# Modulation vectors summed wholly on VectorE, and gate rows spread over the partitions through DRAM

## Chip, cores and metric

One core of one Trainium2 chip. The metric is the device time of the program in microseconds; three runs of a kernel are shown by their median.

## What is computed

Two models run one after the other on 256 tokens of width 1024. The first has two layers of feed-forward, a mixer (state-space, mLSTM and RWKV heads side by side) and feed-forward. The second takes its output and a context of 256 more tokens through two layers. Before each of its parts the rows are normalised, scaled and shifted, and each part's output is multiplied by a gate. All scales, shifts and gates of a layer are the nine parts of one vector of 9216 numbers, and there are two such vectors, one for the tokens (from `c`), one for the context (from `c_ctx`):

```python
silu_c, silu_cc = jax.nn.silu(c), jax.nn.silu(c_ctx)
for l in range(2):
    m_lat = jnp.split(silu_c @ ada_w[l] + ada_b[l], 9)      # ada_w[l]: 1024 x 9216
    m_ctx = jnp.split(silu_cc @ ada_w[l] + ada_b[l], 9)
    def half_ffn(t, m, j):
        h = rmsnorm(t, norm_g[l, j]) * (1 + m[3*j + 1]) + m[3*j]
        return t + 0.5 * m[3*j + 2] * swiglu(h, ...)
    x, ctx = half_ffn(x, m_lat, 0), half_ffn(ctx, m_ctx, 0)
    ...                                                     # Fourier mixing (l=0) or retention (l=1), gated by m[5]
    x, ctx = half_ffn(x, m_lat, 2), half_ffn(ctx, m_ctx, 2)
```

In layer 1 the context ends with retention. Everything is float32. Products are made from a high part and a low part of each operand, three matmuls for one.

## The kernel before

The program is a list of stages (`network`, line 2926): f10 (first feed-forward of layer 0), the mixer, f20, f11, the mixer, f21, then half00, four (Fourier), half02, half10, ret (retention), retout, half12. A stage has phases. `run` in `network` appends a phase to one order, and every engine emits its part of each phase in that order (`Core.run`, 337), so the place of a `run` sets the order on all engines. An engine runs its own queue in order and waits on semaphores of the others. On VectorE and ScalarE each instruction also waits for the one before it.

**Weights.** SyncE loads tiles of 128x2048 (1 MB) into eight places (`Core.fetch`, 319), as each place is released. ScalarE writes the high part of a tile (`split_hi`, line 310), VectorE the low part (`split_lo`, line 316). `Core.plan` puts each split at a position of the order: as early as the target for the high part is free. There are two such targets, three in the stages of 256 rows.

**Feed-forward** (`Ffn`). Each of 22 gate/up tiles is 48 matmuls (line 100), of 256 columns in f10 to f21 and half12 and 512 columns in half00, half02 and half10. Then ScalarE takes Silu of the gate part (line 860), VectorE multiplies by the other part (line 886), ScalarE writes the high part (864) and VectorE the low part (888). The down products follow, in two portions in the stages of 512 columns. `Gated.vector` (710) multiplies the result by the gate and adds it to the rows (712).

**Modulation vectors** (`Ada`). The weights stand with the 1024 inputs on the partitions. A tile holds 4 groups of 128 inputs by 512 outputs; two tiles give 512 outputs. For each group and each of the two vectors VectorE adds weights times one scalar per partition to `acc` (461 for the first, 464 for the rest: `scalar_tensor_tensor`, 128x512). After two tiles TensorE sums `acc` over the partitions, with eight matmuls that have 128 columns of `acc` as weights and a column of ones as input. VectorE adds the bias (`bias`, 474) into `mods`, with outputs on the partitions. The bank that TensorE writes is one that the running stage doesn't use (`ada_bank`), and `clear` makes it wait for the bias add before the bank is used again.

72 tiles are cut into 144 phases of four VectorE instructions, and a last one. `ffn` in `network` puts them between the phases of the feed-forward stages: in f10, f20, f11 and f21 beside two of three gate/up tiles and beside five of the down tiles, 20 in each stage; in half00 two beside every gate/up tile, 44; the rest in half02.

**Gates** (`Gates`). A gate vector is needed along the free dimension, the same on every partition. For each half row of 512 VectorE makes four diagonal 128x128 matrices (667), TensorE multiplies ones by them (four matmuls), and ScalarE copies the bank to `gb` (691). In the feed-forward stages one half row goes behind each of the first tiles.

**Start.** `Setup.scalar` loads the masks and small rows on ScalarE's queue (412 to 415) and takes Silu of the two vectors from the constants (416, 128x16). `Setup.vector` waits for these loads.

## Time and profile before

| | |
|---|---|
| median of 3 runs | 3445.48 us (3442.11 to 3447.05) |
| profiled execution, span | 3442.6 us (the page gives no other time of it) |
| TensorE matmul busy | 3305.7 us, 96% |
| VectorE busy | 2101.4 us, 61% |
| ScalarE busy | 1308.7 us, 38% |
| `scalar_tensor_tensor` of the sum, x504 | 379.0 us |
| first instruction of the sum in a pair of tiles, x72 | 35.1 us |
| DMA | 463.08 MB, mean 135 GB/s |

A busy share is an average over the whole span. Matmuls overlap, so TensorE's 96% doesn't say that it is never waiting. Which engine sets the pace has to be read stage by stage, from the distance between equal instructions and from what ended the idle time in front of them.

### The profile page before, as it was taken

How to read it: one execution, taken by the hardware profiler on the slowest of the kernel's cores; microseconds unless marked ns; L12 is line 12 of the kernel's file. 1: busy time of each engine (PE TensorE's matmuls, PEld its weight loads, DVE VectorE, ACT ScalarE, POOL GpSimd, SP SyncE). 2: the span in 40 equal slices, each digit the busy share in tenths (PEclk: the TensorE clock that was granted, in tenths of full speed). 3: DMA queues.
4: the chain of work that ended last, by engine and by line, in shares of the span. 5: the costliest groups of instructions: out<-in, count | busy, mean ns of one | idle time of the engine just before them, and what ended most of it. 6: DMA issues, size and time to landing. Idle time of an engine off the chain costs nothing.

```text
span 3442.6 us, 47741 instructions
## 1 busy us (share of the span) xinstructions
PE 3305.7 (96%) x19896; PEld 2886.8 (84%) x19896; DVE 2101.4 (61%) x2545; ACT 1308.7 (38%) x1584; POOL 115.9 (3%) x126
## 2 busy tenths in 40 slices
PE   7998999999999899999999999999999999999998
PEld 7988887998988888798888877888878888787897
DVE  6767657777776667678774855763353333544654
ACT  4444244444435234544421223322232222444443
POOL 0001200000000211000000000000000000000000
PEclk9999999999999999999999999999999999999999
DMA  6542021565553022455443531343222222323452
GB/s 247 235 178 74 27 96 67 204 239 197 236 208 117 27 71 74 171 230 217 147 165 122 179 119 38 134 141 104 87 93 90 93 97 73 126 99 109 165 184 98
DMA packets 83842, 463.08 MB, mean 135 GB/s; under 512 B 7573, under 2 KB 11285, under 8 KB 43562
## 3 DMA queue, kind: packets, MB, share of 16 engines
q1 hardware_dynamic: 77952, 451.45, 35.9%
q10 hardware_dynamic: 5674, 8.57, 0.8%
q8 instruction: 157, 2.57, 0.3%
q14 instruction: 59, 0.48, 0.0%
HBM read 458.95 MB, written 1.05 MB: 134 GB/s over the span
## 4 chain that ended last, share of the span: by engine, by line
PE 66%; DVE 24%; ACT 6%; issue 2%; DMA 0%; POOL 0%; DVEq 0%; ACTq 0%; POOLq 0%
PE ps L100 66%; DVE lo L316 8%; DVE acc L464 5%; ACT hi L310 3%; PE ps L557 1%; DVE acc L461 0%; DVE m0restMs L2004 0%; DVE m1restMs L2004 0%; DVE xt L712 0%; DVE ct L712 0%; DVE half00fin L710 0%; DVE f20rot L886 0%; DVE f21rot L886 0%; DVE f10rot L886 0%; DVE f11rot L886 0%
## 5 line engine op out<-in xcount | busy, mean ns | idle before, releaser
L316 DVE TENSOR_TENSOR lo<-raw,hi 128x2048 fp32r<-128x2048 f32 (+1 forms) x357 | 809.6, 2268 | 627.9 <-ACT hi L310 606.2
L310 ACT ACTIVATE hi<-raw 128x2048 fp32r<-128x2048 f32 (+1 forms) x357 | 676.0, 1894 | 578.1 <-PE ps L100 547.5
L464 DVE SCALAR_TENSOR_TENSOR acc<-raw,sil,acc 128x512 f32<-128x512 f32 x504 | 379.0, 752 | 20.4
L100 PE MATMUL ps<-half00hs,hi 128*128 128x512 f32 x672 | 209.4, 393 | 0.9 <-DVE lo L316 0.9
L100 PE MATMUL ps<-half02hs,hi 128*128 128x512 f32 x672 | 209.1, 392 | 1.0 <-DVE lo L316 1.0
L100 PE MATMUL ps<-half10hs,hi 128*128 128x512 f32 x672 | 208.5, 391 | 1.0 <-DVE lo L316 1.0
L100 PEld LDWEIGHTS ps<-half10hs,hi 128*128 128x128 f32 x672 | 125.7, 188 | 28.5 <-DVE lo L316 1.9
L100 PEld LDWEIGHTS ps<-half02hs,hi 128*128 128x128 f32 x672 | 125.5, 188 | 28.6 <-DVE lo L316 1.9
L100 PEld LDWEIGHTS ps<-half00hs,hi 128*128 128x128 f32 x672 | 125.1, 188 | 28.0 <-DVE lo L316 1.8
L100 PE MATMUL ps<-half02hs,lo 128*128 128x512 f32 x352 | 137.9, 392 | 0.0
L100 PE MATMUL ps<-half00hs,lo 128*128 128x512 f32 x352 | 137.6, 391 | 0.0
L100 PE MATMUL ps<-half10hs,lo 128*128 128x512 f32 x352 | 137.5, 391 | 0.0
L100 PE MATMUL ps<-half12hs,hi 128*128 128x256 f32 x704 | 127.2, 283 | 2.1 <-DVE half12hs L636 2.1
L100 PE MATMUL ps<-hi,half00hf 128*128 128x512 f32 x352 | 110.7, 394 | 2.1 <-DVE mods L474 1.4
L100 PE MATMUL ps<-hi,half02hf 128*128 128x512 f32 x352 | 110.4, 394 | 1.5 <-DVE mods L474 1.5
L100 PEld LDWEIGHTS ps<-half12hs,hi 128*128 128x128 f32 x704 | 109.3, 191 | 3.0 <-DVE half12hs L636 1.8
L100 PE MATMUL ps<-hi,half10hf 128*128 128x512 f32 x352 | 109.2, 390 | 0.0
L100 PE MATMUL ps<-f10hs_h,hi 128*128 128x256 f32 x352 | 101.5, 288 | 7.3 <-DVE lo L316 7.2
L100 PE MATMUL ps<-f21hs_h,hi 128*128 128x256 f32 x352 | 100.9, 287 | 5.5 <-DVE lo L316 3.8
L100 PE MATMUL ps<-msk 128*128 128x128 f32 x886 | 104.5, 276 | 1.0 <-PE ps L2819 1.0
L100 PEld LDWEIGHTS ps<-msk 128*128 128x128 f32 x886 | 102.4, 192 | 3.3 <-PE ps L2819 1.2
L100 PE MATMUL ps<-f20hs_h,hi 128*128 128x256 f32 x352 | 100.8, 286 | 3.2 <-DVE f20hs_l L636 1.5
(921 smaller groups left out, 8019.5 us busy)
## 6 DMA issues: line engine op xcount, KB each, us to landing
raw<-in_ffn_w_gate_up SPq DMA_DIRECT2D x88, 1024.0 KB, 9.0
raw<-in_ffn_gu SPq DMA_DIRECT2D x88, 1024.0 KB, 4.8
raw<-in_ffn_w_down SPq DMA_DIRECT2D x85, 1024.0 KB, 5.2
raw<-in_ada_w SPq DMA_DIRECT2D x72, 1024.0 KB, 4.9
raw<-in_w_in_t SPq DMA_DIRECT2D x28, 1024.0 KB, 4.9
raw<-in_ret_w_in SPq DMA_DIRECT2D x24, 1024.0 KB, 4.8
raw<-in_w_out SPq DMA_DIRECT2D x16, 1024.0 KB, 4.9
raw<-in_w_in_n SPq DMA_DIRECT2D x12, 1024.0 KB, 4.8
```

What stands on the lines that cost most here:

```text
L100: return p().matmul(o, l, r, start=start, stop=stop, skip_group_check=True)
L310: a().activation(self.high(w), self.raw[self.place(r)][:, 0:width], ACT.Copy).then_inc(*a.mark(self.wac, w))
L316: v().tensor_tensor(self.low(w), self.raw[self.place(r)][:, 0:width], self.high(w).bitcast(F32), ALU.subtract).then_inc(*v.mark(self.wdv, w))
L464: v().scalar_tensor_tensor(out=acc[:, n, :], in0=w[:, k, :], scalar=s, in1=acc[:, n, :], op0=ALU.mult, op1=ALU.add).then_inc(*v.mark(self. ...
L557: x = p().transpose(b[:, t * 128:(t + 1) * 128], self.xs[:, 2 * s + t, c * 128:(c + 1) * 128], K.ident)
```

## The change

The weights of `Ada` are laid out with the outputs on the partitions: a tile is two groups of 128 outputs by 1024 inputs. The two vectors come as rows of 1024 on every partition (`silb`, loaded by a broadcast of 8 KB to 128 partitions on ScalarE's queue), and Silu is taken there over 128x2048. One `scalar_tensor_tensor` with `accum_out` multiplies 128x1024 weights by a vector and sums over the inputs into one column of `mods`; a phase is two of them. The bias is added once per layer. TensorE has no part in it, nor have the banks and `clear`.

A gate takes one VectorE instruction (`gcol`, 128x16), one DMA per vector from `gcol` to a row in DRAM, where the 8 numbers of a partition go to places 128 elements apart, and one DMA that reads the row back to all partitions. ScalarE issues all of them: the writes in the first of two phases, and in the second it waits for the writes and issues the read. The second phase stands behind the second tile. The other hunks pass the arguments along, number the wait on `mods` by layer, and run two phases for each gate.

```diff
-        self.sil = m.take("sil", 8, 2)
+        self.gcol = m.take("gc", 2, 8)
         self.st = m.take("st", 512)
-        self.acc = m.take("acc", 2, 512)
+        self.silb = m.take("silb", 2, 1024)
+        self.prod = m.take("prod", 1024)
         self.free, self.end = m.at, END
...
-        a().activation(K.sil, K.cc2, ACT.Silu).then_inc(*a.mark(self.ac, "sil"))
+        a().dma_start(K.silb, A["c_c2"].broadcast_to([P, 2048]).rearrange("p (n k) -> p n k",
+                                                                           n=2)).then_inc(*self.c.mark())
+        a.wait_ge(*self.c.all)
+        a().activation(K.silb, K.silb, ACT.Silu).then_inc(*a.mark(self.ac, "sil"))
         yield
...
-    phases = 2 * 2 * 18 * 2 + 1
+    phases = 2 * 36 * 2
     def __init__(self, K, setup):
         super().__init__(K, "ada", "ada")
-        self.setup, self.reduced = setup, 0
+        self.setup = setup
         for i in range(72):
-            l, t, h = i // 36, i // 2 % 18, i % 2
-            self.tiles[2 * i] = [(K.A["ada_w_2"][l, t, h], 2048)]
-        self.banks = []
+            self.tiles[2 * i] = [(K.A["ada_w_2"][i // 36, i % 36], 2048)]
     def vector(self, v):
-        K, acc = self.K, self.K.acc
+        K = self.K
         v.wait_ge(*self.setup.ac["sil"])
         for i in range(72):
-            t, h = i // 2, i % 2
-            w = K.raw[K.place(self.mine[i])].rearrange("p (k n) -> p k n", k=4)
-            for k in range(4):
-                if k % 2 == 0 and (i, k) != (0, 0):
-                    yield
-                if h == 0 and k == 0 and t:
-                    self.bias(v, t - 1)
+            l, t = divmod(i, 36)
+            w = K.raw[K.place(self.mine[i])].rearrange("p (m k) -> p m k", m=2)
+            for m in range(2):
                 v.wait_ge(*K.landed(self.mine[i]))
                 for n in range(2):
-                    s = K.sil[:, 4 * h + k, n:n + 1]
-                    key = ("tile", i) if (k, n) == (3, 1) else ("sum", i, k, n)
-                    if h == 0 and k == 0:
-                        v().tensor_scalar(acc[:, n, :], w[:, k, :], s, None,
-                                          ALU.mult).then_inc(*v.mark(self.dv, *key))
-                    else:
-                        v().scalar_tensor_tensor(out=acc[:, n, :], in0=w[:, k, :], scalar=s, in1=acc[:, n, :],
-                                                 op0=ALU.mult, op1=ALU.add).then_inc(*v.mark(self.dv, *key))
...
+                    key = ("tile", i) if (m, n) == (1, 1) else ("sum", i, m, n)
+                    v().scalar_tensor_tensor(out=K.prod, in0=w[:, m, :], scalar=1.0, in1=K.silb[:, n, :], op0=ALU.mult,
+                                             op1=ALU.mult,
+                                             accum_out=K.mods[:, l, 2 * t + m, n:n + 1]).then_inc(*v.mark(self.dv, *key))
+                if (t, m) == (35, 1):
+                    v().tensor_tensor(K.mods[:, l], K.mods[:, l], bl(K.ab2[:, l, :], 2),
+                                      ALU.add).then_inc(*v.mark(self.dv, "mods", l))
                 yield
-    def clear(self, p):
-        if self.reduced:
-            p.wait_ge(*self.dv["mods", self.reduced - 1])
...
         K = self.K
         for _ in self.rows:
             yield
-        K.ada.clear(p)
         if self.idle:
             if len(self.rows) == 4 and not self.turn[0]:
                 self.before[0].row(p, 0, 1)
...
 class Gates(Stage):
-    def __init__(self, K, who, after, l, j, n, half, gb, dg, bank):
+    phases = 2
+    def __init__(self, K, who, after, before, l, j, n, half, gb):
         super().__init__(K, "gate", who, after)
-        self.l, self.j, self.rows, self.phases, self.half = l, j, 2 * n, 2 * n + 1, half
-        self.gb, self.dg, self.bank = gb, dg, bank
+        self.before, self.l, self.j, self.n, self.half, self.gb = before, l, j, n, half, gb
+        self.row = K.nc.dram_tensor(who + "row", (n, 1024), F32, kind="Internal").ap()
+        self.out, self.back = Loads(K.sem(who + "out"), n), Loads(K.sem(who + "back"))
     def vector(self, v):
+        K, at = self.K, 8 * (3 * self.j + 2)
+        if self.before:
+            v.wait_ge(*self.before.out.all)
+        v.wait_ge(*K.ada.dv["mods", self.l])
+        v().tensor_scalar(K.gcol, K.mods[:, self.l, at:at + 8, :].rearrange("p c n -> p n c"), self.half, None,
+                          ALU.mult).then_inc(*v.mark(self.dv, "gc"))
+        yield
+        yield
+    def scalar(self, a):
         K = self.K
-        self.enter(v)
-        v.wait_ge(*K.ada.dv["mods", 18 * self.l + 17])
-        for i in range(self.rows):
-            n, q = i // 2, i % 2
-            if i:
-                v.wait_ge(*self.pe["sum", i - 1])
-            for m in range(4):
-                c = 8 * (3 * self.j + 2) + 4 * q + m
-                v().tensor_scalar(self.dg[:, m, :], K.ident, K.mods[:, self.l, c, n:n + 1], self.half, ALU.mult,
-                                  ALU.mult).then_inc(*v.mark(self.dv, "dg", i, m))
-            yield
-        yield
-    def tensor(self, p):
-        b = self.K.ps[self.bank]
-        self.enter(p)
-        yield
-        for i in range(self.rows):
-            p.wait_ge(*self.dv["dg", i, 3])
-            if i:
-                p.wait_ge(*self.ac["gb", i - 1])
-            for m in range(4):
-                x = mm(p, b[:, m * 128:(m + 1) * 128], self.K.ones, self.dg[:, m, :])
-            x.then_inc(*p.mark(self.pe, "sum", i))
-            yield
-    def scalar(self, a):
         self.enter(a)
-        yield
-        for i in range(self.rows):
-            n, q = i // 2, i % 2
-            a.wait_ge(*self.pe["sum", i])
-            a().activation(self.gb[:, n, q * 512:(q + 1) * 512], self.K.ps[self.bank][:, :],
-                           ACT.Copy).then_inc(*a.mark(self.ac, "gb", i))
-            yield
+        a.wait_ge(*self.dv["gc"])
+        for n in range(self.n):
+            a().dma_start(self.row[n].rearrange("(c p) -> p c", p=P), K.gcol[:, n, :],
+                          allow_slow_non_contiguous=True).then_inc(*self.out.mark())
+        yield
+        a.wait_ge(*self.out.all)
+        a().dma_start(self.gb, self.row.rearrange("n k -> (n k)").unsqueeze(0).broadcast_to([P, 1024 * self.n]).rearrange(
+            "p (n k) -> p n k", n=self.n)).then_inc(*self.back.mark())
+        yield
     def done(self, e):
-        e.wait_ge(*self.ac["gb", self.rows - 1])
+        e.wait_ge(*self.back.all)
...
         for k, count in enumerate(self.parts):
-            K.ada_bank = 3 if nt == 2 else 7 - 4 * (k % 2)
-            K.ada_bank_free = self.dv["out", k - 1, 3, 1] if k else None
             for j in range(count):
...
+    def rows(w):
+        return np.ascontiguousarray(w.reshape(1024, 36, 2, 128).transpose(1, 3, 2, 0)).reshape(36, 128, 2048)
...
-    d["ada_w_2"] = np.stack([halves(x["ada_w_2"][l]) for l in range(2)])
+    d["ada_w_2"] = np.stack([rows(x["ada_w_2"][l]) for l in range(2)])
...
+    d["c_c2"] = np.concatenate([x["c_2"].reshape(-1), x["c_ctx_2"].reshape(-1)])[None, :]
...
-    nc = _bacc.Bacc("TRN2", target_bir_lowering=False, num_devices=1)
+    nc = _bacc.Bacc("TRN2", target_bir_lowering=False, num_devices=1, dynamic_dma_scratch_size=4096)
```

At the start, ScalarE's queue, from the masks to the first Silu of f10 (`hi_..` is a target of a high part, `raw_..` a place of a loaded tile). Before:

```order
L415 DMA rows<-in_c_rows 128x120
L416 ACT_TABLE_LOAD
L416 ACTIVATE sil<-cols 128x16
L310 ACTIVATE hi_77<-raw_52 128x2048 [waits s_set_act,s_ring3]
L860 ACTIVATE f10rot<-ps 128x256 [waits s_w_hi,s_ffn_pe]
```

Changed:

```order
L415 DMA rows<-in_c_rows 128x120
L416 DMA silb<-in_c_c 128x2048
L419 ACT_TABLE_LOAD
L419 ACTIVATE silb<-silb 128x2048 [waits s_c]
L310 ACTIVATE hi_78<-raw_52 128x2048 [waits s_set_act,s_ring3]
L798 ACTIVATE f10rot<-ps 128x256 [waits s_w_hi,s_ffn_pe]
```

The split of the third weight tile now stands behind a wait for a load.

In f10, VectorE's queue, one tile with a phase of the sum. Before:

```order
L316 TENSOR_TENSOR lo_61<-raw_53,hi_65 128x2048 [waits s_ada_dve,s_w_hi]
L886 TENSOR_TENSOR f10rot<-f10rot,ps 128x256 [waits s_w_lo,s_ffn_act]
L888 TENSOR_TENSOR f10hf_l<-f10rot,f10hf_h 128x256 [waits s_ffn_dve,s_ffn_act]
L464 SCALAR_TENSOR_TENSOR acc<-raw_50,sil,acc 128x512 [waits s_ffn_dve]
L464 SCALAR_TENSOR_TENSOR acc<-raw_50,sil,acc 128x512 [waits s_ada_dve] x3
```

Changed:

```order
L316 TENSOR_TENSOR lo_61<-raw_53,hi_65 128x2048 [waits s_ada_dve,s_w_hi]
L824 TENSOR_TENSOR f10rot<-f10rot,ps 128x256 [waits s_w_lo,s_ffn_act]
L826 TENSOR_TENSOR f10hf_l<-f10rot,f10hf_h 128x256 [waits s_ffn_dve,s_ffn_act]
L456 SCALAR_TENSOR_TENSOR prod,mods<-raw_50,silb 128x1024 [waits s_ffn_dve]
L456 SCALAR_TENSOR_TENSOR prod,mods<-raw_50,silb 128x1024 [waits s_ada_dve]
```

Four instructions of 512 became two of 1024 in the same place.

In four, ScalarE's queue, around the first gate work (`fZ` are the copies behind the first transform, `fxs` the scaled rows of the second half). Before:

```order
L2621 ACTIVATE fxs,st<-ct 128x512 [waits s_four_act] x4
L2586 ACTIVATE fZ<-ps 128x257 [waits s_four_act,s_four_pe] x4
L2606 ACTIVATE fwx_257<-fwx 5x1024 [waits s_four_act,s_four_second]
L691 ACTIVATE four_gb<-ps 128x512 [waits s_four_act,s_gate_pe]
L2628 ACTIVATE fxs<-ct,st 128x512 [waits s_gate_act,s_four_pool]
```

Changed:

```order
L2556 ACTIVATE fxs,st<-ct 128x512 [waits s_four_act] x4
L631 DMA fourgrow<-gc 128x8x1 [waits s_four_act,s_gate_dve]
L631 DMA fourgrow<-gc 128x8x1
L2521 ACTIVATE fZ<-ps 128x257 [waits s_four_pe]
L2521 ACTIVATE fZ<-ps 128x257 [waits s_four_act,s_four_pe] x3
L2541 ACTIVATE fwx_256<-fwx 5x1024 [waits s_four_act,s_four_second]
L635 DMA four_gb<-fourgrow 128x2048 [waits s_four_act,s_fourgout]
L2563 ACTIVATE fxs<-ct,st 128x512 [waits s_four_pool]
```

The wait for the written rows (`s_fourgout`) stands in front of the scaled rows.

## Rows read from the trace of the kernel before

**Rows 1.** The page, busy time by engine and the chain by engine.

```profile
PE 3305.7 (96%) x19896; PEld 2886.8 (84%) x19896; DVE 2101.4 (61%) x2545; ACT 1308.7 (38%) x1584; POOL 115.9 (3%) x126
...
PE 66%; DVE 24%; ACT 6%; issue 2%; DMA 0%; POOL 0%; DVEq 0%; ACTq 0%; POOLq 0%
```

**Rows 2.** VectorE in order of time, f10: start, duration, what [idle before <- releaser].

```profile
39.48 0.42 DVE L886 TENSOR_TENSOR f10rot<-f10rot,ps 128x256 f32<-128x256 f32 x1
...
40.84 3.11 DVE L464 SCALAR_TENSOR_TENSOR acc<-raw,sil,acc 128x512 f32<-128x512 f32 x4
44.06 2.29 DVE L316 TENSOR_TENSOR lo<-raw,hi 128x2048 fp32r<-128x2048 f32 x1
46.45 0.42 DVE L886 TENSOR_TENSOR f10rot<-f10rot,ps 128x256 f32<-128x256 f32 x1
...
49.37 2.29 DVE L316 TENSOR_TENSOR lo<-raw,hi 128x2048 fp32r<-128x2048 f32 x1 [1.58 <-ACT hi L310]
51.76 0.42 DVE L886 TENSOR_TENSOR f10rot<-f10rot,ps 128x256 f32<-128x256 f32 x1
```

**Rows 3.** By tile: ns min/median/max, then first and last start.

```profile
L860 ACT ACTIVATE f10rot<-ps x22: 383/384/388, 28.3 to 164.7; 128x256 f32<-128x256 f32 x22
...
L860 ACT ACTIVATE half12rot<-ps x22: 383/383/385, 3250.9 to 3373.4; 128x256 f32<-128x256 f32 x22
...
L886 DVE TENSOR_TENSOR half10rot<-half10rot,ps x22: 686/689/690, 2568.4 to 2863.9; 128x512 f32<-128x512 f32 x22
...
L886 DVE TENSOR_TENSOR half00rot<-half00rot,ps x22: 686/687/691, 1670.5 to 1988.9; 128x512 f32<-128x512 f32 x22
...
L886 DVE TENSOR_TENSOR half02rot<-half02rot,ps x22: 686/688/690, 2174.4 to 2484.5; 128x512 f32<-128x512 f32 x22
```

**Rows 4.** TensorE in order of time: a reduction in f10, a gate row in half00.

```profile
64.64 1.84 PE L100 MATMUL ps<-msk,acc 128*128 128x1 f32 x16
66.35 0.36 PE L100 MATMUL ps<-f10hs_h,hi 128*128 128x256 f32 x1
...
1682.37 1.05 PE L100 MATMUL ps<-half00dg,msk 128*128 128x128 f32 x8
1683.18 0.48 PE L100 MATMUL ps<-half00hs,hi 128*128 128x512 f32 x1
```

**Rows 5.** Groups by line and shape: count, busy us, mean ns, idle before.

```profile
L100 PE MATMUL ps<-msk,acc 128*128 128x1 f32 x576 | 66.3, 245 | 0.0
...
L464 DVE SCALAR_TENSOR_TENSOR acc<-raw,sil,acc 128x512 f32<-128x512 f32 x504 | 379.0, 752 | 20.4
```

**Rows 6.** Groups by line and shape: VectorE's split of a half tile.

```profile
L316 DVE TENSOR_TENSOR lo<-raw,hi 128x1024 fp32r<-128x1024 f32 x6 | 7.4, 1226 | 46.6 <-ACT hi L310 46.6
```

**Rows 7.** ScalarE in order of time, first norm: read of its accumulator.

```profile
6.24 0.19 ACT L567 ACTIVATION_READ_ACCUMULATOR f10xs<-xt 128x1 f32 x1
```

**Rows 8.** VectorE in order of time, one tile of half00.

```profile
1734.19 0.69 DVE L886 TENSOR_TENSOR half00rot<-half00rot,ps 128x512 f32<-128x512 f32 x1 [2.46 <-ACT half00rot L860]
...
1736.37 6.26 DVE L464 SCALAR_TENSOR_TENSOR acc<-raw,sil,acc 128x512 f32<-128x512 f32 x8
...
1745.34 0.69 DVE L886 TENSOR_TENSOR half00rot<-half00rot,ps 128x512 f32<-128x512 f32 x1 [0.31 <-ACT half00rot L860]
```

**Rows 9.** The chain in order of time, start of f10: start, us, what.

```profile
24.18 6.32 DMA rows<-in_c_rows
```

**Rows 10.** TensorE in order of time, third tile of f10.

```profile
32.87 0.39 PE L100 MATMUL ps<-f10hs_h,hi 128*128 128x256 f32 x1 [1.72 <-DVE lo L316]
```

**Rows 11.** DMA issues (KB each, us to landing), and ScalarE's split by shape.

```profile
raw<-in_ffn_gu SPq DMA_DIRECT2D x88, 1024.0 KB, 4.8
...
L310 ACT ACTIVATE hi<-raw 128x2048 fp32r<-128x2048 f32 x349 | 668.9, 1917 | 523.8 <-PE ps L100 493.4 <-issue 6.0 <-ACT half10hf L864 0.4
```

**Rows 12.** The page, DMA queues: packets, MB, share of 16 engines' span.

```profile
q1 hardware_dynamic: 77952, 451.45, 35.9%
q10 hardware_dynamic: 5674, 8.57, 0.8%
```

More of the change, by code:

```diff
@@ L185, in __init__ @@
         self.ab2 = self.cols[:, c2 + 48:c2 + 192].rearrange("p (l c) -> p l c", l=2)
-        self.cc2 = self.cols[:, c2 + 192:c2 + 208].rearrange("p (c v) -> p c v", v=2)
-        self.heads = self.cols[:, c2 + 208:c2 + 240].rearrange("p (c h) -> p c h", h=8)
+        self.heads = self.cols[:, c2 + 192:c2 + 224].rearrange("p (c h) -> p c h", h=8)
         self.sct = self.st[:, 256:272].rearrange("p (c v) -> p c v", v=2)
@@ L466, in vector @@
-        yield
-        self.bias(v, 35)
-        yield
-    def bias(self, v, t):
-        K, l, c = self.K, t // 18, 4 * (t % 18)
-        v.wait_ge(*self.pe["red", t])
-        v().tensor_tensor(K.mods[:, l, c:c + 4, :], K.ps[self.banks[t]][:, 0:8].rearrange("p (a b) -> p a b", b=2),
-                          K.ab2[:, l, c:c + 4].unsqueeze(2).broadcast_to([P, 4, 2]),
-                          ALU.add).then_inc(*v.mark(self.dv, "mods", t))
-    def tensor(self, p):
-        K = self.K
-        for i in range(73):
-            if i and i % 2 == 0:
-                t = i // 2 - 1
-                self.banks[t:] = [K.ada_bank]
-                b = K.ps[K.ada_bank]
-                p.wait_ge(*self.setup.late.all)
-                p.wait_ge(*self.dv["tile", i - 1])
-                if K.ada_bank_free:
-                    p.wait_ge(*K.ada_bank_free)
-                if t:
-                    p.wait_ge(*self.dv["mods", t - 1])
-                for c in range(4):
-                    for n in range(2):
-                        at = 2 * c + n
-                        x = mm(p, b[:, at:at + 1], K.acc[:, n, c * 128:(c + 1) * 128], K.ones[:, 0:1])
-                x.then_inc(*p.mark(self.pe, "red", t))
-                self.reduced = t + 1
-            yield
-            if i < 72:
@@ L808, in tensor @@
                 yield
-            if nt == 4:
-                K.ada.clear(p)
-            if self.finish.gates:
-                self.finish.gates.done(p)
             if nt == 4 and k:
@@ L2549, in tensor @@
                         p.wait_ge(*self.dv["e", n])
-                    if t == 3:
-                        self.finish.gates.done(p)
                 for h in range(2):
@@ L2948, in fill_to @@
     def fill_to(tiles):
-        while filled[0] < min(4 * tiles + 1, Ada.phases):
+        while filled[0] < min(4 * tiles, Ada.phases):
             fill()
@@ L3090, in half_ffn @@
                                     lambda c, v: K.mods[:, l, 24 * j + c, v:v + 1], (l, j), turn))
-        gates = put(name + "g", Gates(K, name + "g", [norm], l, j, nt // 2, 0.5, gb, dg, 6 if nt == 4 else 3))
+        gates = put(name + "g", Gates(K, name + "g", [norm], latest[0], l, j, nt // 2, 0.5, gb))
+        latest[0] = gates
         s = put(name, Ffn(K, name, norm, Gated(gates, rows, K.at(fin, name + "fin", 2, 512)), A["ffn_gu_2"][l, j // 2],
@@ L3118, in network @@
     ffn(half, gates)
-    gb, dg, rot = K.at(49152, "four_gb", 2, 1024), K.at(57344, "four_dg", 4, 128), K.at(59392, "four_fin", 2, 512)
-    gates = put("fourgates", Gates(K, "fourg", [half], 0, 1, 2, 1.0, gb, dg, 7))
+    gb, rot = K.at(49152, "four_gb", 2, 1024), K.at(59392, "four_fin", 2, 512)
+    gates = latest[0] = put("fourgates", Gates(K, "fourg", [half], latest[0], 0, 1, 2, 1.0, gb))
     four = put("four", Fourier(K, "four", half, 0, both, Gated(gates, both, rot)))
-    for s in (half, half, four, half, half, four, gates, four, gates, four, four, four, gates, four, gates, four, gates):
+    for s in (half, half, four, half, half, four, gates, four, gates, four, four, four, four, four):
         run(s)
@@ L3148, in network @@
     ys = K.split(24576, "ys", 16, 256)
-    gb, dg, rot = K.at(57344, "retgb", 1, 1024), K.at(61440, "retdg", 4, 128), K.at(63488, "retfin", 2, 512)
-    gates = put("retgates", Gates(K, "retg", [ret], 1, 1, 1, 1.0, gb, dg, 3))
+    gb, rot = K.at(57344, "retgb", 1, 1024), K.at(63488, "retfin", 2, 512)
+    gates = latest[0] = put("retgates", Gates(K, "retg", [ret], latest[0], 1, 1, 1, 1.0, gb))
     rout = put("retout", Out(K, "retout", [ret], A["ret_w_out_2"][0], yT, ys, Gated(gates, K.xa, rot), 6))
@@ L3157, in network @@
         run(rout)
-        if q < 3:
+        if q < 2:
             run(gates)
@@ L3308, in layout @@
     cc += [col(x["norm_g_2"]), col(x["ada_b_2"])]
[L3309 removed]
+    d["c_c2"] = np.concatenate([x["c_2"].reshape(-1), x["c_ctx_2"].reshape(-1)])[None, :]
     heads = (np.arange(8)[None, None, :] == 2 * np.arange(4)[None, :, None] + np.arange(128)[:, None, None] // 64)
     heads = heads.astype(np.float32)
[L3312 removed]
+    d["c_cols"] = np.ascontiguousarray(np.concatenate(cc + [heads.reshape(128, 32)], 1))
     d["c_spread"] = np.ascontiguousarray(heads.transpose(2, 1, 0)).reshape(8, 512)
```

19 lines of the change are left out of this document (7 added, 12 removed).

## The prediction

> **What bounds the kernel now.** I read the page first. TensorE is busy for 96% of the span, but the chain that ended last lies on VectorE for 24% [rows 1], so somewhere VectorE sets the pace. The part of it that the change touches is the summing of the modulation vectors. To see who leads there, I read VectorE in order of time in the first feed-forward stage (f10). A gate/up tile that carries a piece of that sum takes 46.45 - 39.48 = 6.97 us from one `f10rot` product to the next, and four instructions of the sum with one split fill 5.4 us of it. A tile without a piece takes 51.76 - 46.45 = 5.31 us [rows 2]. That second figure is itself a loop: VectorE's product, ScalarE's high part of it, ScalarE's split of the next weight tile (1.92 [rows 11]), VectorE's split (2.29), and again the product; VectorE's 1.58 us of idling there is the wait for ScalarE. Two tiles of three carry a piece, so three tiles take 2 x 6.97 + 5.31 = 19.25 us, and 21 intervals 135 us; the first and last Silu of f10 stand 136.4 us apart [rows 3]. Stage half12, with the same products and no pieces, needs 122.5 us, or 5.83 a tile [rows 3]. So **the four stages of the first block (f10, f20, f11, f21) go at VectorE's pace while they carry pieces, not at TensorE's.**
>
> In half00 (512 rows in place of 256) a tile carries two pieces and takes 11.15 us, with VectorE waiting 0.31 us for TensorE's result [rows 8]: TensorE leads by a hair. Half10 has the same products without pieces: 295.5 us from first to last product, against 318.4 in half00 and 310.1 in half02 [rows 3].
>
> **What goes from TensorE.** A reduction (8 matmuls, 16 records) holds it from 64.64 to 66.35, or 1.71 us; one row of a gate from 1682.37 to 1683.18, or 0.81 us [rows 4]. There are 576 / 16 = 36 reductions [rows 5] and 20 gate rows (four each in half00, four, half02 and half10, two each in ret and half12). All of it is 61.6 + 16.2 = 78 us of TensorE time. It counts in full only where TensorE leads.
>
> **What VectorE's sum costs after.** A phase was four instructions of 128x512, 752 ns each [rows 5], 40.84 to 44.06 = 3.22 us with gaps [rows 2]. It becomes two `scalar_tensor_tensor` over 128x1024 with an accumulated output. No row shows that on VectorE. The lower end is a two-input instruction of the same size without a sum: 1.226 us [rows 6]. For the read of the accumulator the nearest row is ScalarE's, 0.19 us, part of which overlaps there [rows 7]. That gives S between 1.23 and 1.42; gaps can make it 1.45. The upper end is that the two inputs and the sum go at half rate: a 2048-element pass, 2.29 us [rows 2]. I take **S = 1.30**, near the lower end, because the same instruction with two float32 inputs in SBUF already ran over 512 elements in 752 ns and not in twice that [rows 5].
>
> The Trainium skill speaks against this change: "Vector Engine (DVE) Microarchitecture Reference", in "Points that are easy to get wrong", says that this instruction form with two non-bf16 SBUF sources runs at half throughput, since both read ports are taken and none is left to read the accumulator back. For the form without the sum the trace disagrees (752 ns for 512 elements); for the form with it no row decides. By the rule the sum would come out as the first rival below.
>
> **Stage by stage.**
> - f10, f20, f11, f21: a tile with a piece becomes 6.97 - 3.22 + 2 x 1.30 + 0.07 = 6.42 us, so 0.55 less; 14 of them in the 21 intervals give 7.7 us. The other 5 of a stage's 20 pieces lie beside the down products, where TensorE leads: 1.25 reductions, 2.1 us. Three tiles then take 2 x 6.42 + 5.31 = 18.15 us, still above TensorE's 17.5 (3 x 5.83), so the reductions removed from the gate/up part give nothing themselves. 9.8 x 4 = **-39.3**.
> - half00: VectorE's tile is 11.15 - 0.31 - 6.26 (the eight instructions [rows 8]) + 4 x 1.30 = 9.78 us, and TensorE's share is 11.15 less half a reduction, 10.29. TensorE leads clearly, so the stage falls to half10's time less the gates: 295.5 - 4 x 0.81 = 292.3. **-26.1**. The same for half02: 310.1 - 292.3 = **-17.8**. Their waits for the bank and the bias add are in these differences, with the diagonals on VectorE.
> - gates in half10, four, ret, half12: 4 + 4 + 2 + 2 rows of 0.81: **-9.6**.
> - The start. ScalarE now waits for the copy of the two vectors (1 MB over 128 partitions) and takes Silu over 2048 elements before it splits the third weight tile. The chain waits there until 24.18 + 6.32 = 30.50 for the last small load [rows 9], and TensorE waits for the split behind it [rows 10]. The new load stands behind that one. A 1 MB load lands 4.8 us after its issue [rows 11]; in a full queue only its own transfer counts. Between 0 and 4.8, I take half, 2.4 us. Silu is priced as ScalarE's pass of that size, 1.9 [rows 11], the split another 1.9, and VectorE's split starts at 30.5 + 2.4 + 3.8 + gaps = 37.2 where it started at 30.5. f10 is paced by VectorE from there, so nothing is won back: **+6.7**.
> - The trip through DRAM. ScalarE issues the writes in one phase and waits for them in the next, and behind that wait stand weight splits and, in four, the scaled rows of the second half. A write is 1024 elements of 4 bytes, each apart from its neighbours in DRAM. Cheapest: a packet at the ACT queue's mean, 0.008 x 16 x 3442.6 / 5674 = 78 ns, so for two rows 2048 / 16 x 0.078 = 10 us. Dearest: at the SP queue's mean, 0.359 x 16 x 3442.6 / 77952 = 254 ns, so 32 us [rows 12]. The ACT mean is for larger packets and should overstate 4 bytes. A tile of half00 hides 10 us. In four only four short copies and one conversion stand between; ret and half12 write one row. I take **+2** in all, for four. The broadcast back is needed tens of us later.
>
> The Trainium skill, "DMA: Bandwidth & Descriptors", "Rules for kernel authors", warns of just this write: a last dimension that isn't contiguous lowers to one descriptor per element, and it says to rearrange. That is why I priced it by packets; no row here shows such a write.
>
> The emptier SBUF slots, the smaller scratch and the 16 columns less of constants cost nothing that is waited for: the weight loads keep their order and places, ahead of use.
>
> **Sum.** -39.3 - 26.1 - 17.8 - 9.6 + 6.7 + 2 = -84.1 us against the profiled span of 3442.6, so 3358.5. The page gives that execution's span and no other time of it; the median of the three runs stands 2.9 us above, which I carry over: **3361 us**.
>
> **Rivals.**
> 1. *The accumulating pass runs at half rate*, S = 2.29. In the first block's stages a tile with a piece takes 6.97 - 3.22 + 0.07 + 4.58 = 8.40 us: 14 x 1.43 - 2.1 = +17.9 a stage, +71.6. In half00 a tile is 4.58 + 9.16 = 13.74 against 11.15: +57 over 22, and +25.9 over ten of half02. With -9.6 and +8.7: +154, **about 3599**. It decides from S = 1.7 us, where the sum is near zero. For it: two full-width inputs. Against: 752 ns. Chance 0.07.
> 2. *The element writes are slow*, at 32 us for two rows. ScalarE stands 22 us in each of half00, half02 and half10, 28 in four, about 9 and 10 in ret and half12, and TensorE runs out of split weights: +113 on -86, **about 3472**. It needs more than some 25 us. Against: the ACT queue's mean. Chance 0.03.
> 3. *Gain partly eaten*: S = 1.45 (f stages +16.8, halves +5) and writes of 10 to 15 us exposed in four (+10): **about 3393**. Chance 0.18.
> 4. *Several small debts cancel the gain*, S near 1.65: 3445. Chance 0.02.
>
> The forecast itself has 0.70; its best corner (S = 1.24, load hidden at the start, four's diagonals gone from its chain) gives some -97, 3349. About 0.2% (7 us) is what a measurement of this kernel tells from none: faster 0.88, within 0.02, slower 0.10. The range takes in cases 0 and 3 with room for what the stage sums miss: 3338 to 3412.
>
> **What would show it.** The new VectorE row: 1.2 to 1.3 us plus a short read (right), above 1.7 (rival 1). First to last Silu: f10 near 129 us, f20 near 126 to 127, half00 292 to 293. TensorE's first long wait at the start growing from 1.7 to about 8 us. ScalarE's idle time put down to the gate writes: none in the halves, a few us in four. Wrong if the halves stay above 300, or if f stages fall to half12's 120 (then the loop isn't what paces them).

## The result and the profile after

The changed kernel takes **3422.8 us** (median of four runs, 3418.0 to 3426.0) against 3444.2 us for the kernel before in the same runs (3442.1 to 3447.1): ratio 0.9938, 95% interval 0.9924 to 0.9952. That is 21 us faster. I had forecast 84, to 3361, and the measured time lies outside my range of 3338 to 3412. The profiled execution has a span of 3422.5 us against 3442.6.

The page first, busy times and chain, against [rows 1]:

```profile
PE 3253.3 (95%) x19160; PEld 2806.0 (82%) x19160; DVE 2015.4 (59%) x2437; ACT 1298.5 (38%) x1564; POOL 115.9 (3%) x126
...
PE ps L100 63%; DVE lo L316 9%; DVE prod L456 5%; ACT hi L310 3%; PE ps L514 1%; DMA half00grow<-gc 0%; DMA half02grow<-gc 0%; DMA retgrow<-gc 0%; DMA fourgrow<-gc 0%; DMA silb<-in_c_c 0%; DMA half12grow<-gc 0%; DVE m0restMs L1942 0%; DVE m1restMs L1942 0%; DVE ct L656 0%; DVE xt L656 0%
```

TensorE's busy time fell by 52 us. In the chain there are now five of the six writes of gate rows and the load of the two vectors, which the chain of before doesn't have.

**The sum is what I took it for.** VectorE's groups over the whole span (busy time, then mean ns of one):

```profile
L456 DVE SCALAR_TENSOR_TENSOR prod<-raw,silb 128x1024 f32<-128x1024 f32 x288 | 352.9, 1225 | 15.0
L456 DVE DVE_READ_ACCUMULATOR prod<-raw,silb 128x1 f32 x288 | 23.7, 82 | 0.0
```

and VectorE in order of time in f10, against [rows 2]:

```profile
49.64 0.42 DVE L824 TENSOR_TENSOR f10rot<-f10rot,ps 128x256 f32<-128x256 f32 x1
...
51.00 1.23 DVE L456 SCALAR_TENSOR_TENSOR prod<-raw,silb 128x1024 f32<-128x1024 f32 x1
52.15 0.08 DVE L456 DVE_READ_ACCUMULATOR prod<-raw,silb 128x1 f32 x1
52.27 1.22 DVE L456 SCALAR_TENSOR_TENSOR prod<-raw,silb 128x1024 f32<-128x1024 f32 x1
...
53.61 2.29 DVE L316 TENSOR_TENSOR lo<-raw,hi 128x2048 fp32r<-128x2048 f32 x1
56.00 0.42 DVE L824 TENSOR_TENSOR f10rot<-f10rot,ps 128x256 f32<-128x256 f32 x1
...
61.31 0.42 DVE L824 TENSOR_TENSOR f10rot<-f10rot,ps 128x256 f32<-128x256 f32 x1
```

From 51.00 to 53.61 two sums take 2.61 us, 1.30 each; from one sum to the next it is 1.27. This tile with a piece takes 56.00 - 49.64 = 6.36 us, the one before it 6.44, one without 5.31. These are the figures of the forecast (6.42 and 5.31).

**The gate rows are not.** ScalarE at the first tiles of half00:

```profile
1643.15 0.60 ACT L798 ACTIVATE half00rot<-ps 128x512 f32<-128x512 f32 x1 [5.44 <-PE ps L100]
1644.50 0.63 ACT L802 ACTIVATE half00hf<-half00rot 128x512 fp32r<-128x512 f32 x1 [0.76 <-DVE half00rot L824]
1651.29 1.01 ACTq L631 DMA_DIRECT2D half00grow<-gc  x2
1652.35 1.92 ACT L310 ACTIVATE hi<-raw 128x2048 fp32r<-128x2048 f32 x1 [7.22 <-issue]
1654.36 0.60 ACT L798 ACTIVATE half00rot<-ps 128x512 f32<-128x512 f32 x1
1657.41 0.63 ACT L802 ACTIVATE half00hf<-half00rot 128x512 fp32r<-128x512 f32 x1 [2.46 <-DVE half00rot L824]
1668.39 0.34 ACTq L635 DMA_DIRECT2D half00gb<-half00grow  x1
1668.77 1.91 ACT L310 ACTIVATE hi<-raw 128x2048 fp32r<-128x2048 f32 x1 [10.73 <-DMA half00grow<-gc]
```

ScalarE stands still twice. First 7.22 us ahead of the write: it waits for `gc`, and the same stretch on VectorE shows that `gc` (at 1651.04) comes right behind the last of four sums of this tile:

```profile
1649.77 1.22 DVE L456 SCALAR_TENSOR_TENSOR prod<-raw,silb 128x1024 f32<-128x1024 f32 x1
1650.92 0.08 DVE L456 DVE_READ_ACCUMULATOR prod<-raw,silb 128x1 f32 x1
1651.04 0.17 DVE L621 TENSOR_SCALAR gc<-mods 128x16 f32<-128x16 f32 x1
1654.30 2.29 DVE L316 TENSOR_TENSOR lo<-raw,hi 128x2048 fp32r<-128x2048 f32 x1 [3.08 <-ACT hi L310]
```

Then 10.73 us at the write itself. Behind both waits stands the split of the next weight tile, for which TensorE waits. ScalarE's waits at the other writes (us in total, times, longest):

```profile
ACT hi L310 <- DMA retgrow<-gc: 11.1, 1, 11.1
...
ACT hi L310 <- DMA half02grow<-gc: 10.5, 1, 10.5
...
ACT fxs L2563 <- DMA fourgrow<-gc: 9.0, 1, 9.0
```

It was 6.8 us in half12 and 3.0 in half10. The issues of these writes by the view of DMA issues (KB each, median us from issue to landing):

```profile
half00grow<-gc ACTq DMA_DIRECT2D x2, 4.0 KB, 15.4
fourgrow<-gc ACTq DMA_DIRECT2D x2, 4.0 KB, 10.9
half02grow<-gc ACTq DMA_DIRECT2D x2, 4.0 KB, 15.3
half10grow<-gc ACTq DMA_DIRECT2D x2, 4.0 KB, 12.1
retgrow<-gc ACTq DMA_DIRECT2D x1, 4.0 KB, 12.9
half12grow<-gc ACTq DMA_DIRECT2D x1, 4.0 KB, 12.0
```

**The start.** ScalarE there, where before it split the third tile 24.18 + 6.32 us into the span [rows 9]:

```profile
24.70 0.45 ACTq L416 DMA_DIRECT2D silb<-in_c_c  x1
...
36.77 1.91 ACT L419 ACTIVATE silb<-silb 128x2048 f32<-128x2048 f32 x1 [10.30 <-DMA silb<-in_c_c]
38.77 1.91 ACT L310 ACTIVATE hi<-raw 128x2048 fp32r<-128x2048 f32 x1
```

The load lands 12.0 us after its issue, and VectorE's split comes at 40.77 instead of 30.52. TensorE, in the same place:

```profile
43.12 0.58 PE L100 MATMUL ps<-f10hs_h,hi 128*128 128x256 f32 x1 [12.21 <-DVE lo L316]
```

The account by stage, in changes against before. Each stage goes from its norm's first copy out of PSUM on ScalarE to that of the next stage; f10's comes at 15.7 us, and what lies ahead of it is counted in the last row. The retention's output product is in ret:

| | before, us | forecast | after | e3 | e5 |
|---|---|---|---|---|---|
| f10 with the start | 213.5 | -3.1 | +1.1 | +1.2 | -9.2 |
| f20, f11, f21 | 631.8 | -29.4 | -27.0 | -27.0 | -27.7 |
| two mixers | 790.6 | 0 | -1.0 | -6.1 | +0.7 |
| half00, four | 503.5 | -27.3 | -5.8 | -23.9 | -23.8 |
| half02 | 394.3 | -17.8 | -3.5 | -12.6 | -12.7 |
| half10 | 379.4 | -3.2 | +3.4 | +3.0 | +2.8 |
| ret | 311.9 | -1.6 | +11.3 | +1.2 | +1.0 |
| half12 and the first 15.7 us | 217.5 | -1.6 | +1.5 | -4.0 | -4.0 |
| span | 3442.6 | -84.0 | -20.1 | -68.2 | -72.9 |

The first block came out as forecast; the missing 64 us lie where gates are written, in half10, and at the start. (e3 and e5 are experiments below. The mixers moved by a few us from one execution to another in kernels that are alike there.)

### The profile page after: what moved, and what is told of

Its sections match the earlier page's. It is cut to its first block, busy times and chain, and to the rows that moved or that the text cites. A ratio compares the mean times of both kernels' runs of the same rounds, so it can differ in the third digit from the quotient of the medians.

```text
span 3422.5 us, 46059 instructions
## 1 busy us (share of the span) xinstructions
PE 3253.3 (95%) x19160; PEld 2806.0 (82%) x19160; DVE 2015.4 (59%) x2437; ACT 1298.5 (38%) x1564; POOL 115.9 (3%) x126
## 3 DMA queue, kind: packets, MB, share of 16 engines
q10 hardware_dynamic: 17082, 14.90, 1.5%
## 4 chain that ended last, share of the span: by engine, by line
PE 63%; DVE 24%; ACT 7%; DMA 3%; issue 2%; ACTq 0%; DVEq 0%; POOL 0%; POOLq 0%
PE ps L100 63%; DVE lo L316 9%; DVE prod L456 5%; ACT hi L310 3%; PE ps L514 1%; DMA half00grow<-gc 0%; DMA half02grow<-gc 0%; DMA retgrow<-gc 0%; DMA fourgrow<-gc 0%; DMA silb<-in_c_c 0%; DMA half12grow<-gc 0%; DVE m0restMs L1942 0%; DVE m1restMs L1942 0%; DVE ct L656 0%; DVE xt L656 0%
## 5 line engine op out<-in xcount | busy, mean ns | idle before, releaser
L456 DVE SCALAR_TENSOR_TENSOR prod<-raw,silb 128x1024 f32<-128x1024 f32 x288 | 352.9, 1225 | 15.0
```

Source lines behind the costliest of these rows:

```text
L456: v().scalar_tensor_tensor(out=K.prod, in0=w[:, m, :], scalar=1.0, in1=K.silb[:, n, :], op0=ALU.mult, op1=ALU.mult, accum_out=K.mods[:, l, ...
```

## Experiments

Times are medians, ratios those to the kernel before, run beside each (3443.3 to 3444.6 us for e1 to e10).

| | us | ratio, 95% |
|---|---|---|
| changed kernel | 3422.8 | 0.9938 (0.9924 to 0.9952) |
| e1 sum alone | 3395.7 | 0.9859 (0.9842 to 0.9875) |
| e2 gates alone | 3467.8 | 1.0068 (1.0053 to 1.0083) |
| e3 write earlier, wait later | 3379.1 | 0.9810 (0.9795 to 0.9825) |
| e4 small descriptor scratch | 3445.3 | 1.0003 (0.9994 to 1.0013) |
| e5 e3, vector load waited for later | 3371.8 | 0.9788 (0.9773 to 0.9802) |
| e6 e5 with 4 KB of padding | 3370.4 | 0.9781 (0.9767 to 0.9796) |
| e7 before, tiles moved | 3443.8 | 0.9998 (0.9989 to 1.0007) |
| e8 changed, writes in runs of 32 bytes | 3387.4 | 0.9829 (0.9812 to 0.9845) |
| e9 e5, writes in runs of 32 bytes | 3368.0 | 0.9782 (0.9769 to 0.9796) |
| e10 e5, two more filler products | 3369.9 | 0.9787 (0.9771 to 0.9802) |

**e1 and e2: one half of the change each.** e1 keeps the diagonals and products for the gates (the old `Gates` class with its phases), e2 keeps the old sum and takes the new gates:

```diff
 # e2, in Gates
...
-                v().tensor_scalar(self.dg[:, m, :], K.ident, K.mods[:, self.l, c, n:n + 1], self.half, ...)
-                x = mm(p, b[:, m * 128:(m + 1) * 128], self.K.ones, self.dg[:, m, :])
...
+        v().tensor_scalar(K.gcol, K.mods[:, self.l, at:at + 8, :].rearrange("p c n -> p n c"), self.half, ...)
...
+            a().dma_start(self.row[n].rearrange("(c p) -> p c", p=P), K.gcol[:, n, :], ...)
```

> VectorE's sum as changed, gates by diagonals and products as before. Theory A (the trip of the gate rows through DRAM, 11 to 15 us a write, blocks ScalarE and eats the gain): everything but the start behaves as forecast; f20, f11, f21 9 us shorter each, half00 about 22 and half02 about 14 us shorter, f10 about even, the time about 3382 us. Theory B (the new sum itself slows TensorE: 512-column matmuls stand 0.70 us per three instead of 0.68 in the changed kernel): the half stages gain only half of that and show 0.70, the time above 3400.

> Gate rows through DRAM, the sum as before, scratch of 4096 bytes as in the change. Theory A: 16 us of gate matmuls go, some 45 us of waits come; slower than before, about 3470 us, with ScalarE waiting 10 us or more for the gate write in half00, half02, four and ret. Theory B: no such loss, about 3430 us.

Measured 3395.7 and 3467.8. The sum alone is worth 49 us, the gates alone cost 23, and together that is -26 against the -21 measured for both. So the half of the change that takes 16 us of TensorE's work away (20 rows of 0.81 [rows 4]) makes the kernel slower by itself. e2 came out near its first theory (3470). e1 met neither of its two: it is 14 us above the 3382 of theory A, and its three 512-row stages show the 0.70 us per three products of theory B (last experiments below), though its time stayed under theory B's 3400. In e2's half00 the same two waits stand, 8.18 and 7.25 us:

```profile
1683.72 1.92 ACT L311 ACTIVATE hi<-raw 128x2048 fp32r<-128x2048 f32 x1 [8.18 <-issue]
...
1696.67 1.92 ACT L311 ACTIVATE hi<-raw 128x2048 fp32r<-128x2048 f32 x1 [7.25 <-DMA half00grow<-gc]
```

**e3: the waits taken off the path.** The gate's first phase goes ahead of the tile's sums, and three more tiles lie between the write and the wait for it. In four and ret, whose lines aren't shown here, the later phases of the gate move back in the same way.

```diff
-    phases = 2
+    phases = 5
@@ ffn
                 run(s)
                 if s.nt == 4:
+                    if gates:
+                        run(gates.pop(0))
                     fill(2)
...
-                if gates and j >= late:
+                if s.nt == 2 and gates and j >= late:
@@ Gates.scalar
-        yield
+        for _ in range(4):
+            yield
         a.wait_ge(*self.out.all)
```

> The changed kernel with the write issued ahead of the tile's pieces of the sum and the wait for it three phases later (four tiles behind the write in place of one). Theory A: ScalarE no longer waits for the gate writes, and half00, half02, half10, four, ret and half12 give back about 40 us together: 3380 to 3390 us. Theory B: no change against the changed kernel, about 3423 us.

Measured 3379.1, 44 us less than the changed kernel. ScalarE in half00 now:

```profile
1641.24 1.54 ACTq L631 DMA_DIRECT2D half00grow<-gc  x2
1642.82 1.92 ACT L310 ACTIVATE hi<-raw 128x2048 fp32r<-128x2048 f32 x1 [2.59 <-issue]
...
1685.06 0.34 ACTq L636 DMA_DIRECT2D half00gb<-half00grow  x1
```

The writes still take 9.4 to 12.8 us by the median, 0.9 to 4.7 less than in the changed kernel, but ScalarE no longer waits for any of them, and the Silus of half00's first tiles are 11.1 to 11.2 us apart where the changed kernel has 16.4 and 15.3 for its second and third.

**e8: the price of single elements.** Only the destination of the write changes; the row's columns then stand in another order, so the result is not the reference's, while the work is the same:

```diff
-            a().dma_start(self.row[n].rearrange("(c p) -> p c", p=P), K.gcol[:, n, :],
+            a().dma_start(self.row[n].rearrange("(p c) -> p c", p=P), K.gcol[:, n, :],
```

> The changed kernel, with the gate row written so that the 8 values of a partition lie side by side (128 runs of 32 bytes a row in place of 1024 of 4 bytes); the row's columns then stand in another order, so each gate column multiplies with another column's value: the work is the same. Theory: the 11 to 15 us of the write are the price of its single elements; it lands in 2 to 4 us, ScalarE's waits at it (10.7 in half00, 9.0 in four, 11.1 in ret, 6.8 in half12) go, and of e3's 44 us some 20 to 30 come back: 3393 to 3403. The rest stays, since the write is still queued behind VectorE's pieces. Rival: the time is a fixed cost of a write and the read back, whatever the size of its runs: landing 10 us or more, and 3418 to 3426.

Measured 3387.4, 35 us less than the changed kernel with the same bytes and the same order of work; I had expected 20 to 30. The issues:

```profile
half00grow<-gc ACTq DMA_DIRECT2D x2, 4.0 KB, 4.6
fourgrow<-gc ACTq DMA_DIRECT2D x2, 4.0 KB, 1.5
half02grow<-gc ACTq DMA_DIRECT2D x2, 4.0 KB, 4.5
half10grow<-gc ACTq DMA_DIRECT2D x2, 4.0 KB, 3.0
retgrow<-gc ACTq DMA_DIRECT2D x1, 4.0 KB, 1.9
half12grow<-gc ACTq DMA_DIRECT2D x1, 4.0 KB, 2.8
```

and what is left in half00:

```profile
1655.04 1.92 ACT L310 ACTIVATE hi<-raw 128x2048 fp32r<-128x2048 f32 x1 [7.04 <-DVE gc L621]
...
1661.19 1.92 ACT L310 ACTIVATE hi<-raw 128x2048 fp32r<-128x2048 f32 x1 [0.46 <-ACT half00hf L802]
```

The wait at the write has gone; the one behind VectorE's sums stays, at 7.04 us. It goes in e3, and e3 is 8 us faster than e8. By the account of stages, half00 with four is 4.8 us shorter in e3 than in e8 and half02 3.9.

The packet records of the trace say where the time of a write is. In the changed kernel's half00 the queue has 2080 packets of 4 bytes (2048 of them the elements), 9 ns each, and all of them lie between 1655.20 and 1656.40 us; but the rows land at 1665.40 and 1668.37, 14.1 and 16.7 us after their issues. In e8 the last packet of the two rows ends at 1658.48 and they land at 1658.85 and 1659.14. So the single elements cost time behind their packets and not in them. What happens there no run shows.

**e5: the load at the start.** e3, with the wait and Silu moved out of `Setup` into the sum's own first phase, and the first pieces placed later:

```diff
 # Setup.scalar
-        a.wait_ge(*self.c.all)
-        a().activation(K.silb, K.silb, ACT.Silu).then_inc(*a.mark(self.ac, "sil"))
 # Ada.scalar
+        a.wait_ge(*self.setup.c.all)
+        a().activation(K.silb, K.silb, ACT.Silu).then_inc(*a.mark(self.ac, "sil"))
 # ffn
-                elif j % 3 < 2:
+                elif j % 3 < 2 and filled[0] + j > 1:
```

> The kernel of e3 with the vector's load waited for later: ScalarE waits for it, and takes its Silu, in the sum's own first phase, and the first two pieces of the sum (of f10's tiles 0 and 1) are laid to a later tile; what is computed is the same. Theory: in the changed kernel ScalarE stands 10.3 us at that load with the third tile's rounding behind it, and that goes on to TensorE as 10 us of idle time and some half clock after it; then the first Silu is back near 28 to 30 us and the time falls from 3379 to 3369 (3365 to 3373). Rival: the load's 12 us only trade places with the ring's own loads, which are slow at the start anyway, and the wait comes back two tiles later: 3376 to 3382.

Measured 3371.8, in the expected range and 7 us less than e3. The first Silu of f10 is at 28.47 us again, and TensorE's long wait is 2.00 us where it was 12.21. The stage with the start is 10.4 us shorter (table, 1.2 + 9.2), and the mixers were longer in this execution.

**e4, e6, e7, e10: what is left in the halves.** e5 has no wait for a gate or a load on its path, and still half00 needs 297.5 us from first to last Silu and half02 296.6, not the 292.3 of the forecast; half10 needs 296.9, with fewer products than before (295.5 [rows 3]). Three 512-column products (two with the high part of the weights, one with the low) repeat after 0.68 us in the kernel before, at most of half10's tiles, and after 0.70 us in e5 at all of them. TensorE of before, then of e5, both late in half10:

```profile
2805.00 0.62 PE L100 MATMUL ps<-half10hs,hi 128*128 128x512 f32 x2
2805.45 0.39 PE L100 MATMUL ps<-half10hs,lo 128*128 128x512 f32 x1
2805.68 0.62 PE L100 MATMUL ps<-half10hs,hi 128*128 128x512 f32 x2
```

```profile
2740.47 0.63 PE L100 MATMUL ps<-half10hs,hi 128*128 128x512 f32 x2
2740.94 0.39 PE L100 MATMUL ps<-half10hs,lo 128*128 128x512 f32 x1
2741.17 0.63 PE L100 MATMUL ps<-half10hs,hi 128*128 128x512 f32 x2
```

The distance is 0.68 against 0.70 us, at a granted clock of 1.00 in half10's stretches of both. Over a stage it is some 4 to 5 us, and there are three such stages. I tried the addresses (e4: descriptor scratch of 4096 in the kernel before, which moves all tiles down by 12 KB; e7: that and 8 KB of padding; e6: e5 with its stage tiles put back to where they lie before, less 64 bytes) and the place of the instructions in TensorE's stream (e10).

```diff
 # e7, on the kernel before, with dynamic_dma_scratch_size=4096 as in e4
+        self.pad = m.take("pad", 2, 1024)
 # e6, on e5
+        self.pad = m.take("pad", 1024)
 # e10, on e5, ahead of half02 and of half10
-    norm.idle = 0, 17
+    norm.idle = 0, 18
-    norm.idle = 0, 22
+    norm.idle = 0, 23
```

> The kernel before with the DMA scratch cut to 4096 bytes, which moves every tile in SBUF by 12 KB. If the place of the tiles sets the spacing of the matmuls, the 512-column gate/up matmuls stand 0.70 us per three here too and the time is 5 to 10 us above before; if not, 0.68 and the same time, about 3444 us.

> e5 with 4 KB of unused on-chip memory behind the product's scratch tile, so that the stages' tiles lie again at the addresses that they have in the kernel before (only the first five ring slots and two rounded tiles stay 12 KB lower). Theory: TensorE's 512-column products are spaced 0.70 us per three in every tile of the changed kernel, and 0.68 in most tiles of before, because of where their operands lie; then the mean product in half10 falls from 395 to 391 or 392 ns, the half stages by 3 us each and the time by 8 to 12 us against e5. Rival: the spacing has nothing to do with addresses, and the time is e5's within 3 us.

> The kernel before, its tiles moved to the addresses of the changed kernel (smaller descriptor scratch, 8 KB unused behind the accumulators), nothing else. Theory of addresses: the products' mean in half10 goes from 391 to 395 ns, its first-to-last Silu from 295.5 to 297 to 301 us, and the time from 3444 to 3450 to 3456. Rival: no effect, 3442 to 3447 and 391 ns.

> e5 with one more of the small filler products ahead of half02's norm and one more ahead of half10's, nothing else; half00 is left as it is, for comparison. Theory: the 0.70 us per three 512-column products that the changed kernel shows in place of 0.68 depends on where the stage's instructions lie in TensorE's stream, which the removed products moved; then half02 or half10 or both change their spacing (mean product 391 to 393 ns in place of 395, first-to-last Silu 293 to 295 us in place of 297) and half00 does not. Rival: the spacing belongs to something else, and all three stages keep 395 ns and 297 us.

Nothing moved: e4 and e7 keep the 391 ns and 295.5 us of before in half10, e6 and e10 the 395 ns and 296.9 us of e5. So shifts of the tiles by 12 KB and 4 KB do nothing, nor does a shift of the instructions by one or two products.

The theory of addresses doesn't fall with that, because these edits miss the changed kernel's addresses by 64 bytes. The change takes 16 columns (64 bytes) out of the constants, which lie below the stages' tiles. By the programs' memory maps half10's normalised rows (`half10hs`) start at byte 101248 of a partition before, at 88960 in e4 and 97152 in e7, but at 97088 in the changed kernel and 101184 in e6; e2, which has 64 bytes more than before, has them at 89024. The beat goes with this offset in every kernel of the study. With none (before, e4, e7) three 512-column products take 0.68 us in most tiles and 0.70 in the rest. With 64 bytes less (the changed kernel, e1, e3, e5, e6, e8, e9, e10) they take 0.70 everywhere. In e2 they take a third value, 0.69, in all tiles of half00 and half02 and all but the first five of half10. The 256-column products go the other way: three repeat after 0.36 us in half12 before, e4 and e7, and after 0.34 or 0.35 in all others. No run changes the 64 bytes alone, so this is the candidate that is left and not a cause that is shown.

**e9: all together.** e5 with e8's short writes and the gate columns of weights and bias stored in the matching order:

```diff
...
+    for j in (2, 5, 8):
+        perm[j] = perm[j].reshape(128, 8).T
...
     def rows(w):
+        w = w[:, perm]
...
+    cc += [col(x["norm_g_2"]), col(x["ada_b_2"][:, perm])]
```

> e5 with the gate columns of the weights and of their bias stored in another order, so that a partition's 8 gate values are neighbours in the row and the write goes out as 128 runs of 32 bytes, with the right values in the right columns. Theory: after e3's order and e5's start the path holds no wait at a write any more, so the short write gives nothing or little: 3366 to 3372. Rival: the 1024-element writes still delay other transfers (the ring's weights, the mixers' loads), and the time falls by 5 us or more, to 3366 or below, as e8's did by 35.

Measured 3368.0. The writes land in 1.5 to 2.9 us, and against e5 the difference is within the intervals, so the first theory holds: off the path the length of a write costs nothing that can be seen here. It has the lowest median of the study, within the intervals of e5, e6 and e10: 2.2% (2.0 to 2.3) faster than the kernel before and 55 us faster than the changed one.

## Why the prediction was wrong, point by point

- **S = 1.30: right.** 1225 ns, a read of 82 ns, 1.27 us from one to the next and 1.30 to the split behind them. Rival 1 fell. The rule of the Trainium skill that I quoted from "Vector Engine (DVE) Microarchitecture Reference", "Points that are easy to get wrong", does not agree with the trace as I read it: at half throughput the 1024 elements would take twice the 1.23 us of a plain two-input pass, and they take the same.
- **f10, f20, f11, f21: right.** Tiles of 6.36 and 6.44 us in turn were forecast as 6.42; the first-to-last Silus are 126.9, 126.3, 127.0 and 128.2 us. Three stages gave 27.0 us of 29.4.
- **The start: mis-sized.** I took 2.4 us for what the load adds behind the last small one. The load took 12.0 us from issue to landing, not 4.8, with the ring's own loads moving at that time, and f10 with the start lost 4.2 us more than forecast. The load landed at 24.70 + 12.04 = 36.74, 6.2 us behind the 30.50 at which the last small load of before landed; that is the term of 2.4. e5 shows the whole debt as 10.4 us of that stage, forecast as 6.7. The reading "half of its landing time" was what failed here: 4.8 was a median of loads from the other queue over the whole span, and I put it in a stretch in which the DMA engines are busy for 85% (last section).
- **The trip through DRAM, +2: the step that failed.** It had two parts. First, the write was priced at 78 ns a packet over 16 engines, 5 us a row and 10 for two. One row takes 12 to 13 us, and two take 11 to 15 by the median (of two values, so their mean), so the time doesn't double with the rows. e8 shows that the single elements are the price, since the same bytes in runs of 32 land in 1.5 to 4.6. But it isn't packet time: the recorded packets take 9 ns each, and in half00 the rows land 9 and 12 us after the last of them. The forecast's 10 us, near the measured size, came by luck from the wrong mechanism. The rule of the Trainium skill in "DMA: Bandwidth & Descriptors", "Rules for kernel authors" (one descriptor per element) agrees with the trace: ScalarE's queue has 17082 packets in the changed kernel and 8122 in e8, and the difference of 8960 is that of ten rows of 1024 elements and ten of 128 runs.

  Second, "a tile of half00 hides 10 us" was wrong, because I counted the tile's length and not what ScalarE has to do between the write and the wait. The write itself was issued 7 us late, behind VectorE's four sums, and from it to the wait's place there were only 1651.29 to 1658.04 us, 6.7. Even the write of 10 us that I had priced would have shown by some 3 us. I had priced the phase's DMA and not the one VectorE instruction in front of it, which the program puts behind the sums. So the path was wrong: +2 in four alone was forecast, and ScalarE stood 51 us at the writes in all (10.7 in half00, 9.0 in four, 10.5 in half02, 3.0 in half10, 11.1 in ret, 6.8 in half12). e3 gives 44 us back, of the 64 that are missing; e8 shows 35 of them with the elements, and the order gives 8 more.
- **Rival 2 (slow writes, 32 us for two rows, 3472) named the place** and the mechanism but asked for more than some 25 us. It decides from far less: at 11 to 15 us all six places already stand still. Rival 3 had 10 us exposed in four alone.
- **Halves at 292.3: wrong even with the waits gone.** e5's 297.5, 296.6 and 296.9 show that half10's floor moved itself, from 295.5 minus four gate rows to 297. That is a term that I had at nothing: the forecast says that the smaller scratch and the 16 columns less of constants cost nothing. It is 14.6 us over the rows of the three stages (3.5 + 5.1 + 6.0 by the table). Its form is the slower beat of the 512-column products, some 4.6 us a stage. half12 gained by its faster beat, 4.0 us in e5 where I had 1.6. The cause of both is open; the offset of 64 bytes goes with them and is untested.
- **TensorE's share in half00: misread, without effect on the sum.** I took half a reduction from the tile of 11.15 us [rows 8], to 10.29. TensorE's reductions before and after that tile start at 1719.79 and 1744.51 us, so it holds almost nothing of one, and its neighbours take 13.6 and 12.7 us. TensorE's share is 10.9 to 11.15, what such tiles take in that stage; it leads all the more, and the stage was priced by half10.
- **What the forecast said would show it wrong** did: the halves stayed above 300 (306.0 and 306.1 us in half00 and half02), and ScalarE's idle time at the gate writes was 10.73 us in half00 where I had said none.

## What to carry to other kernels

Work taken off the bounding engine is worth what is left after the longest wait that the replacement puts on an engine which feeds it: follow the replacement's first instruction through its own queue, the one that it is issued from and the one that prepares its data, and count only the work that stands between issue and wait as cover. A small scattered write of 4-byte elements landed here after 11 to 15 us, where the median load of a megabyte takes 4.8; lay the source so that neighbours stay neighbours, or wait for it several tiles later. And a load's duration is to be read from the same stretch of the span, not from a median.

## What the runs showed of the hardware

A write of one row of 1024 single float32 elements from SBUF to DRAM landed 12.0 and 12.9 us after its issue in the changed kernel (10.1 at the least, in e5), two rows by their median 10.9 to 15.4 (9.2 in e2 and 9.1 in e6 at the least), and as 128 runs of 32 bytes 1.5 to 4.6 in e8 and 1.5 to 2.9 in e9. The read back of 512 KB or 1 MB behind it took 6.1 to 9.0 us in the changed kernel and 3.5 to 6.2 in e8, but 4.5 to 8.4 in e3 with single elements and 3.7 to 7.1 in e9 with runs, so the form of the write isn't shown to set it.

VectorE's product with a summed output took no longer than a plain two-input pass: 1225 ns over 1024 elements against 1226 for a subtraction of that size [rows 6], and the read of the accumulator, 82 ns, lies partly beside it (it starts at 52.15, and the product ends at 52.23).

At the start TensorE idled for 12.21 us, and by the windows of the changed kernel (us, TensorE, weight loads, VectorE, ScalarE and GpSimd busy, then the granted clock) its clock was at 0.50, the 1.2 GHz level, in the 12 us in which it came back, where before it was at 1.00:

```profile
24.00:36.00 12.00, 6.90 (x60) 6.59 (x58) 1.12 (x1) 1.28 (x1) 0.00 (x0) 0.96 0.85 332
36.00:48.00 12.00, 4.88 (x23) 4.89 (x24) 6.37 (x8) 6.92 (x6) 0.00 (x0) 0.50 0.00 0
```

What the lower clock cost by itself was not separated: f10's tiles are paced by VectorE from there. The same rows show the transfers at 332 GB/s, the DMA engines busy for 85%, while the vector's load was in flight, and none in the 12 us after it: SyncE issued one weight load at 25.29 and the next at 53.53 (25.43 and 43.98 before), since the places of the ring were full and TensorE released none.
